# A hybrid retention and SSD layer on eight cores: values of all heads in one projection, gates as columns, first loads by quarters, the shift between the last half sums, and the last tile in pieces

## The reference

```python
h    = x * (1 + sc1) + sh1                       # sh1, sc1, g1, sh2, sc2, g2 = split(silu(cond) @ w_ada + b_ada)
proj = h @ w_in                                  # q, k, v, g (retention), z, x|B|C, dt (SSD)
o_ret = silu(g) * rms_norm(bidir_scan(q, k * dk**-0.5, v, v, lg_f, lg_b, ...))   # 4 heads of 128; rotary on latent q, k
xbc  = silu(depthwise_conv(x|B|C))               # 5 taps
o_ssd = rms_norm((bidir_scan(C, B, xs*dt_f, xs*dt_b, ...) + d_skip*xs) * silu(z)) * ssd_norm_w
x = layer_norm(ALPHA * x + g1 * (concat(o_ret, o_ssd) @ w_out))
x = layer_norm(ALPHA * x + g2 * ((silu(h2 @ w_gate) * (h2 @ w_up)) @ w_down))    # h2 = x * (1 + sc2) + sh2
```

## Time and profile before

| | us |
|---|---|
| median of 3 runs (lowest to highest) | 722.16 (721.06 to 725.79) |
| the profiled execution | 722.71 |
| its span on the slowest core (core 3) | 721.7 |
| spans of the eight cores | 710.6 to 721.7 |

### The profile page before, as it was taken

One profiled execution on the slowest core, in us unless ns is written; L12 is line 12 of the kernel. 1 busy time (PEld: TensorE's weight loads), 2 busy tenths in 40 slices (PEclk: granted clock), 3 DMA queues, 4 the chain that ended last, 5 costly groups with the idle time before them and its releaser, 6 DMA issues.

```text
span 721.7 us, 13394 instructions; the slowest of 8 cores (710.6 to 721.7 us)
## 1 busy us (share of the span) xinstructions
PE 674.9 (94%) x4248; PEld 345.7 (48%) x4248; DVE 396.1 (55%) x803; ACT 328.3 (45%) x514; POOL 350.5 (49%) x390
## 2 busy tenths in 40 slices
PE   0799999998989999999999999999999999999993
PEld 0244764643548445446565455444444444444441
DVE  2888358652578936887786885212122112466444
ACT  2381876786655535858786445111111110132221
POOL 2520416322524769867773321986471000397764
PEclk9999899999998999999999999999999999999997
DMA  8999897997573398754079647684689954021112
GB/s 249 339 282 143 130 164 132 206 198 244 109 212 90 74 153 169 134 98 93 16 170 215 149 147 132 112 161 77 148 149 167 266 141 81 0 89 66 58 53 88
DMA packets 26677, 102.93 MB, mean 143 GB/s; under 512 B 3168, under 2 KB 7264, under 8 KB 21744
## 3 DMA queue, kind: packets, MB, share of 16 engines
...
## 4 chain that ended last, share of the span: by engine, by line
PE 81%; DMA 8%; DVE 4%; issue 4%; ACT 1%; POOL 1%; SPq 1%; DVEq 0%; POOLq 0%; ACTq 0%
PE psum L708 79%; DMA arena<-cstf 6%; DVE arena L756 2%; DMA arena<-sssd 2%; PE psum L711 2%; ACT arena L733 1%; DVE arena L790 1%; DVE arena L781 1%; POOL arena L756 1%; SPq L194 1%; DVE arena L770 0%; DVE psum L1400 0%; POOL arena L194 0%; ACT L733 0%; DVE arena L764 0%
## 5 line engine op out<-in xcount | busy, mean ns | idle before, releaser
L708 PE MATMUL psum<-arena 128*128 128x512 bf16 (+7 forms) x4152 | 664.5, 317 | 34.4 <-ACT arena L733 21.1
L708 PEld LDWEIGHTS psum<-arena 128*128 128x128 bf16 (+2 forms) x4152 | 334.6, 100 | 361.0 <-issue 83.8
L756 POOL TENSOR_TENSOR arena<-arena 128x512 f32<-128x512 f32 (+5 forms) x220 | 279.7, 1289 | 167.4 <-DVE arena L764 67.1
L733 ACT ACTIVATE arena<-psum 128x512 bf16<-128x512 f32 (+3 forms) x208 | 118.7, 579 | 187.0 <-PE psum L708 172.1
L733 ACT ACTIVATE arena<-arena 128x512 bf16<-128x512 f32 (+8 forms) x159 | 110.1, 713 | 164.4 <-DVE arena L770 86.5
L756 DVE TENSOR_TENSOR arena<-arena,psum 128x512 bf16<-128x512 bf16 (+1 forms) x120 | 81.0, 685 | 144.8 <-PE psum L708 132.2
L756 DVE TENSOR_TENSOR arena<-psum,arena 128x512 bf16<-128x512 f32 (+4 forms) x182 | 111.4, 635 | 66.7 <-PE psum L708 62.7
L733 ACT ACT_TABLE_LOAD x52 | 66.7, 1283 | 22.3 <-PE psum L708 11.5
L194 POOL DMA_DIRECT2D arena<-w_gu x44 | 25.9, 588 | 80.6 <-PE psum L708 75.7
L756 DVE TENSOR_TENSOR arena<-arena 128x1 f32<-128x1 f32 (+9 forms) x105 | 51.4, 498 | 22.8 <-POOL arena L756 14.2
L770 DVE SCALAR_TENSOR_TENSOR arena<-arena 128x512 f32<-128x512 f32 (+1 forms) x72 | 49.4, 695 | 4.1 <-DVE arena L756 0.9
...
## 6 DMA issues: line engine op xcount, KB each, us to landing
...
arena<-w_ada POOLq DMA_DIRECT2D x10, 1024.0 KB, 12.6
...
arena<-xT SPq DMA_DIRECT2D x6, 1024.0 KB, 25.8
...
arena<-w_ada SPq DMA_DIRECT2D x4, 1024.0 KB, 25.3
```

The source lines that it names most:

```text
L708: return P.add({PE: (c, lambda e: e.matmul(R(out), lhsT=R(lhsT), rhs=R(rhs), start=start, stop=stop))}, [lhsT, rhs], [out])
L733: fn = lambda e: e.activation(out=R(out), in_=R(in_), func=func, **{k: R(v) for k, v in kw.items()})
L756: fn = lambda e: e.tensor_tensor(out=R(out), in0=R(in0), in1=R(in1), op=op)
```

## The change

- Values: w_in's 512 value columns become a fourth slab w_in3, loaded once behind w_in2, and `v_proj` makes v for all heads with the tokens stationary (eight 128x512 matmuls a tile), for the context behind `z_proj(GA)` and for the latents behind `z_proj(GB)`. A head's weights are now w_qk (256 columns) and w_g (128).
- Gates: `gate_row` calls `mod_cols` (128x2 matmuls), transposes the eight columns (4 transposes in all), copies and stores them; `gate_load` reads in two halves.
- First loads: `part_load` with quarters (w_ada2 by column halves, xT, w_in0, w_in1 by two k-tiles), the first halves of xT for the latents ahead of w_ada3, `cstf` and `smalls` later, casts on ScalarE and VectorE only. Scale sums in three parts, with bias and 1 added in one instruction.
- The shift's sums get level 0.35 instead of 0.6, which puts them between the last half sums of `proj_xbc`; sums of the context that wait for the second quarter may take their bank early.
- The last tile: `last_tile` sums 512, 256 and 256 columns, with squares and row sums by piece, and a shorter end of its norm.
- Rings: no v ring, g 2 to 1 and scaled keys 2 to 1 for the latents, y2 3 to 2. EV 3 to 2 (the table's load behind context head 2), HG (3, 6) to (2, 5) (which FFN step releases the latents' head weights). LEVELS and PLACED are new.

```diff
-LEVELS = {('blk0', 1.4): -0.05, ('blk1', 1.4): 0.02, ('blk10', 1): 0.3, ('blk11', 1): -0.1, ('blk2', 1.4): 0.02,
+LEVELS = {('blk0', 1.4): -0.7, ('blk10', 1): -0.22, ('blk11', 1): 0.02, ('blk4', 1.4): -0.4, ('blk6', 1.4): 0.1,
...
-XA, HG, EV, LB, LZ, LMB, NSF = 3, (3, 6), 3, 1.6, 1.55, 1.32, 3
+XA, HG, EV, LB, LZ, LMB, NSF = 3, (2, 5), 2, 1.6, 1.55, 1.32, 3
...
+    def part_load(name, dst, src, c0, n, after=()):
+        s = P.buf("%s_f%d" % (name, c0), n)
+        o = P.dma(SP, s, src[:, c0:c0 + n], after=after)
+        for i in range(0, n, 1024):
+            cp(dst[:, c0 + i:c0 + i + 1024], s[:, i:i + 1024], (ACT, DVE))
+        return o
...
+    for q in range(2):
+        f = P.buf("ada2_f%d" % q, 2048)
+        f3 = f.rearrange("p (k n) -> p k n", k=8)
+        P.dma(SP, f3, w_ada_d[2].rearrange("p (k n) -> p k n", k=8)[:, :, q * 256:q * 256 + 256])
+        for i in range(2):
+            cp(a2[q][:, i * 4:i * 4 + 4, :], f3[:, i * 4:i * 4 + 4, :], (ACT, DVE))
+        xT_load(2, 0, q * 1024, 1024)
+        part_load("w_in0", w0, w_in_d[0], q * 1024, 1024)
+        part_load("w_in1", w1, w_in_d[1], q * 1024, 1024)
+    xT_load(0, 0)
+    xT_load(1, 0)
+    for q in range(2):
+        part_load("ada3", ada[3][0], w_ada_d[3], q * 2048, 2048)
+    xT_load(2, 1)
...
-    chain = [xTo[(0, 1)], xTo[(1, 1)]]
+    chain = [o_w1, xTo[(0, 1)], xTo[(0, 1)]]
...
-    P.level = 0.6
+    P.level = 0.35
     for half in range(2):
         sh1[half] = mod_cols("sh1_%d" % half, half, "mod")
...
-                            ps = P.ps("start")
+                            ps = P.ps("start", 512, ck == 2 and q == 0)
...
+    w_in[3] = next_slab("w_in3", w_in_d[3])
...
     def gate_row(which, half):
...
-        for kt in range(8):
-            o = mm(ps[0:2, :], scv3[:, kt, :], wv[:, kt, :], kt == 0, kt == 7)
...
+        m = mod_cols("gc%d%d" % (which, half), (4, 10)[which] + half, "dense")
+        P.level = 1.2
+        ps = P.ps("dense", 128)
+        o = tr(ps[0:8, :], gc[(which, half)])
...
+    def v_proj(g):
+        P.tag = "v%d" % g
+        for t in TT[g]:
+            ps, o = tm(w_in[3][0], t)
+            v_tm[t] = P.buf("v%d" % t, 512, BF16)
+            cp(v_tm[t], ps, (ACT, DVE))
...
-            for j in range(4):
-                for kt in range(8):
-                    o = mm(ps[:, j * 128:(j + 1) * 128], hT3[ck][:, kt, j * 128:(j + 1) * 128], w[1][:, kt, 0:128], kt == 0, kt == 7)
...
+    def last_tile(t, pool, lv, gate):
+        ck, o_ = t // 4, (t % 4) * 128
+        s = P.buf("sL", 16)
+        u, v = P.buf("uL", 1024), P.buf("vL", 1024)
+        for i, (c0, n) in enumerate(((0, 512), (512, 256), (768, 256))):
+            cs = slice(c0, c0 + n)
+            P.level = lv
+            ps = P.ps(pool, n)
+            for ft in range(22):
+                mm(ps, aT[(ft, ck)][:, o_:o_ + 128], wd[(c0 // 512, ft // 11)][:, ft % 11, c0 % 512:c0 % 512 + n], ft == 0, ft == 21)
+            P.level = LV_EV
+            tt(u[:, cs], ps, gate[:, cs], ALU.mult)
+            stt(u[:, cs], x1[t][:, cs], ALPHA, u[:, cs], ALU.mult, ALU.add, accum_out=s[:, i:i + 1])
+            act(rjn()[:, 0:n], u[:, cs], AF.Square, scale=1.0 / 32.0, accum_out=s[:, 3 + i:4 + i])
...
+        ts(s[:, 8:9], s[:, 6:7], s[:, 2:3], ALU.add, -1.0 / 1024.0, ALU.mult)
+        stt(s[:, 9:10], s[:, 8:9], s[:, 8:9], s[:, 7:8], ALU.mult, ALU.subtract)
+        for half in range(2):
+            hs = slice(half * 512, half * 512 + 512)
+            stt(v[:, hs], u[:, hs], s[:, 8:9], ln2[:, hs], ALU.add, ALU.mult)
+        ts(s[:, 10:11], s[:, 5:6], s[:, 9:10], ALU.subtract)
+        tt(s[:, 11:12], s[:, 10:11], mhalf[:, 0:1], ALU.pow, POOL)
+        for half in range(2):
+            hs = slice(half * 512, half * 512 + 512)
+            stt(v[:, hs], v[:, hs], s[:, 11:12], ln2[:, 1024 + half * 512:1536 + half * 512], ALU.mult, ALU.add)
+            P.dma(SP, y_d[t * 128:(t + 1) * 128, hs], v[:, hs], is_out=True)
```

150 lines of the change are left out of this document (73 added, 77 removed), and 7 rows, old and new, of the table LEVELS.

## The result

The changed kernel takes 727.44 us (median of 9 runs, 725.87 to 729.59) beside 722.16 for the kernel before. The ratio is 1.0062, with a 95% interval of 1.0044 to 1.0079: 0.6% slower, where 700.3 had been forecast and 690 to 715 given as the range. A second measurement of the same kernel (the control among the experiments) gives 1.0064. Medians are over all executions of a kernel, while the ratios leave out those in which the cores of one die ran slower at a lower clock.

The account below looks back on a forecast made before the run. TensorE, busy 94% of the span, was taken as the bound, with 46.8 us idle and losses at the lower clock. Terms 7.5 + 1.1 + 5.9 + 2.6 + 2.3 + 2.5 = 21.9 gave 700.3 us, range 690 to 715.

Parts of the forecast that it names:

- Start: Start: the same bytes loaded in another order bring the convolution at 69.7 instead of 77.2 us, -7.5 (0 to -9.5).
- the clock there: Convolution's first 2.3 us at the lower clock: half is won because TensorE is busy before it, -1.1 (0 to -1.5).
- The rival that blamed the size of the quarters: Start: small first loads of 512 KB don't land faster, the start's gain is gone, 710.1 us; chance 0.12.
- So this load decides: Start: the load of the second halves, ready at 43.1 us, sets the pace whichever clock the first matmuls get.
- Values in one projection: Value matmuls: 384 of 128 columns at 0.069 us become 96 of 512 at 0.215, -5.9 (0 to -9.0).
- gates: Gates as columns: 32 matmuls of 512 go, 128 two-column ones and four transposes come, -2.6 (-3.2 to +2.8).
- weight loads show: Rival on the short value matmuls: each waited for its own 100 ns weight load, term 17.8, 688.4 us; chance 0.08.
- The rotary table: Middle: the table's earlier load saves half of its wait and the lower clock behind it, -2.5 (0 to -5.0).
- the lead is given back in the middle: Rival: loads set the middle's pace, so the start's 8.6 and the table's 2.5 us go, 711.4 us; chance 0.20.
- Last tile: Tail: the last tile in pieces leaves 9.3 instead of 11.6 us behind the last matmul, -2.3 (-1.1 to -3.7).
- Rings and priorities: Single or shorter rings (g, scaled keys, y2) and new priorities: hidden behind other matmuls, counted at nothing.
- The slower rival: Heads and blocks: single rings stall the heads, seven waits of 5.0 us give 735.3 us; chance 0.07.

Follow-up runs that it names:

- long_runs: Changed kernel with the first scale slab's two loads in rows of 8 KB instead of 1 KB pieces (scale wrong, only times count): 723.03 us, ratio 1.0033.
- run 88: Not a follow-up run: the words say that TensorE had executed 88 of its 194 matmuls by 44.73 us on the changed kernel's slowest core.
- const_early: Changed kernel with the constants' loads behind the first quarters and three of GpSimd's loads behind its ten diagonal products: 723.1 us, ratio 1.0029.
- five_edits: Changed kernel with const_early, two_moved, mod_earlier_2, tile 6's norm products on VectorE, first scale slab in k-tile halves with 8 KB rows: 710.66 us, ratio 0.9855.
- short_values: Changed kernel with each of the 96 value matmuls of 512 columns split in place into four of 128: 731.36 us, ratio 1.0131.
- mod_earlier_2: Changed kernel with the sh2 and sc2 slabs some ten places earlier in GpSimd's list, all buffers but four at its addresses: 722.51 us, ratio 1.0023.
- two_moved: Changed kernel with two long VectorE instructions, whose results are wanted much later, put some places later in VectorE's list: 722.67 us, ratio 1.0026.
- start_before: Changed kernel with the whole start of the kernel before (loads, casts, diagonals, scale sums, level 0.6): 722.95 us, ratio 1.0029.
- the four cures: Edits of the changed kernel in const_early, long_runs, two_moved and mod_earlier_2, singly worth 0.35, 0.31, 0.38 and 0.41% against the control's 1.0064.

## Why the prediction was wrong, step by step

**Start, -7.5, and the clock there, -1.1: it was +5.9.** Four of its steps failed.

- "These land at 12.1 ... the matmul starts at 13.2": it came at 15.3 on the mean (15.41 on the slowest core). The rate of 3.25 us a MB was taken from rows of 8 KB and applied to pieces of 1 KB. By all eight cores it is 14.7 and 14.6 in the two profiles of the changed kernel, and with long rows 13.9 and 14.1. So the short rows are about 0.6 of the miss; even with long ones w_in0's first quarter lands at 12.9, not 12.1. The rival that blamed the size of the quarters had the right symptom and the wrong cause. By the Trainium skill (DMA: Bandwidth & Descriptors, Measured) batches are to be of 1 MiB and more; long_runs shows no loss by loads of 512 KB that follow one another in a queue (11.2 MB at 40.1, and 40.5 with 1 MB loads).
- "So this load decides", the second halves at 43.1: w_in0's second half landed at 45.8 and 44.1 on the mean of the two profiles, 42.9 before, and that is the smaller part. On the slowest core TensorE had run 88 of its 194 matmuls by 44.73, stood until 48.94 for VectorE, took the next 40 at a lower clock (11.44 us instead of 8.6), and waited again for 1.31. I had counted TensorE and the loads, and not VectorE, which scales, casts and empties the banks for it; nor that the constants' later load, which I mentioned nowhere in the sum, sets when GpSimd's ten products run. const_early shows it: 2.7 us, with that load itself no earlier (45.8). long_runs takes another 2.7.
- "Two of the three waits at the shift go ... one of 1.2 us stays": all three are there, 2.68 together, and one of 1.31 ahead of them. "Two slabs behind MB 14.2" took the slabs to be issued when the queue allows. They hang on an xT load, which lands 3.5 to 4.8 us later than before, and on VectorE's work behind it, and the MB 14.2 comes 2.6 to 3.6 later; the second slab landed at 75.53 on the slowest core (71.1 to 76.1 on the others) instead of 64.8.
- The clock: half of the 2.3 us at the lower level behind the convolution's first matmul was to go, "Now TensorE is busy from 43.1 but for 1.2 us". That premise failed with the waits. On the slowest core the lower level lasts from 83.5 to 88.5 there, 5.0 us, and it comes in the start too: cold is 4.2 there, before 1.4. Two windows of the changed kernel (busy and count of PE, PEld, DVE, ACT and POOL, granted clock, DMA share, GB/s):

```profile
84.00:86.00 2.00, 2.00 (x13) 1.37 (x10) 1.14 (x4) 1.50 (x2) 1.71 (x9) 0.50 0.93 193
86.00:88.00 2.00, 2.00 (x12) 1.42 (x11) 0.00 (x0) 1.13 (x3) 2.00 (x18) 0.50 0.64 72
```

With const_early and long_runs together the convolution comes at 75.3. What parts that from 69.7 was not taken apart further; the scalings of the latents' x beside GpSimd's products, seen in five_edits, are one piece of it. In the sum itself only the gates' upper end is a slip: +2.8 should be about +2.6.

What the prediction named as a sign of error, a convolution later than 75, came: 83.

**Values in one projection, -5.9, and gates, -2.6: -7.5 for both, with 8.5 forecast.** The sum is nearly right, the inside of the first term is not. The 0.069 us of a 128-column matmul was mis-sized: in a row they start 0.0555 apart, so the length gives 0.6. The 81 ns of the Trainium skill (TensorE: Matmul & The Clock Gate, Back-to-back issue gap) are further off. The gates' 32 wide matmuls for 128 tiny ones and four transposes give 6.9 - 3.2 - 0.4 = 3.3. By count that is 3.9, and the table's work falls by 3.5. The other 4.0 are small delays. Part of them lies where TensorE changes between 512 and 128 columns: before, some 30 of 219 changes a core are late, 3.3 us together, and after, 4 of 145. But the other 189 changes of before keep the plain distance, so the turns between values and projections are not a cost by themselves; what makes those 30 late stays open, and no run brought the alternation back alone. The rival "weight loads show" is out: in short_values they start 0.056 apart, not 0.100.

**The rotary table, -2.5, "the other waits of the middle I leave as they are".** The table's wait went, as forecast, and the second half of the sentence failed: waits 11.2 to 18.7, cold 5.2 to 6.7. In place of the wait of 3.42 stands one for a slab of w_ada, which the change had made later itself (150.54 instead of 116.14), and in the new order work that TensorE needs stands behind VectorE's stretched products. mod_earlier_2 and two_moved are each worth 3.5 us of waits (1.9 against the control). Here the rival "the lead is given back in the middle" is right in part: of start_before's 6.1 us only 2.4 arrive on the slowest core, and some 3.7 on the mean core.

**Last tile, -2.3: -1.4** (10.6 from TensorE's end, 9.3 forecast). The sum took each step at its length alone. Two VectorE steps lasted 1.75 beside GpSimd's products; with those on VectorE it is 9.8, and 0.5 of my sum of short steps was too little.

**Rings and priorities, at nothing.** The waits read above end on loads and on VectorE's and ScalarE's work, and none was traced to a ring; but no ring was lengthened to try it, so this zero is not shown. The slower rival named rings, and the four cures account for the slowdown without them.
